# Delta-rule branch of a two-layer decoder step: which side products run whole, where the output products stand between the chain's steps, and the order of four small steps

## The reference

```python
def rwkv7_scan(r, w, k, v, kk, a, S0):
    def step(S, xs):
        r_t, w_t, k_t, v_t, kk_t, a_t = xs
        sa = jnp.einsum('bhvk,bhk->bhv', S, -kk_t)
        S = (S * w_t[:, :, None, :] + sa[..., None] * (kk_t * a_t)[:, :, None, :]
             + v_t[..., None] * k_t[:, :, None, :])
        y = jnp.einsum('bhvk,bhk->bhv', S, r_t)
        return S, y
...
    y = head_groupnorm(y, ln_w, ln_b)
    y = y + jnp.sum(r_h * k_h * rk, axis=-1, keepdims=True) * v_h
    return y.reshape(B, T, RWKV_W) * g, S, p_rwkv[:, -1, :]
```

## Time and profile before

| | |
|---|---|
| median of 3 runs | 2676.49 us (2673.93 to 2677.24) |
| the profiled execution's own time | 2676.28 us |
| its span in the trace | 2674.5 us |
| TensorE busy | 2612.9 us, 98% of the span |
| VectorE busy | 846.5 us, 32% |
| ScalarE busy | 581.3 us, 22% |
| delta stage, layer 0 | 415 to 741 us of the span |
| delta stage, layer 1 | 1497 to 1823 us |
| TensorE's waits for L1588 (`bonus_sum`) | 5.1 us in 14 waits |
| TensorE's waits for L1662 (`level_w`) | 4.1 us in 18 waits |
| one middle pass of the loop | 39.5 us (x 12; the first and the last pass of each layer differ) |

### The profile page before, as it was taken

How to read it: one execution, slowest core, us unless ns; L and a number is a source line. 1 busy time by engine, 2 the same in 40 slices (tenths; PEclk the granted TensorE clock), 3 DMA queues, 4 the chain that set the end, 5 groups by cost and what they waited for, 6 DMA issues and landing times. The chain is left out here.

```text
span 2674.5 us, 81765 instructions
## 1 busy us (share of the span) xinstructions
PE 2612.9 (98%) x36178; PEld 2063.5 (77%) x36178; DVE 846.5 (32%) x2419; ACT 581.3 (22%) x1731; POOL 0.2 (0%) x4
## 2 busy tenths in 40 slices
PE   8999999999999999999999999999999999999998
PEld 5777886666677777677777666667799999999997
DVE  2022665556511000202266556561311111111111
ACT  2232333333211000112333333321111111111111
POOL 0000000000000000000000000000000000000000
PEclk9999999999999999999999999999999999999999
DMA  6333442222243434342354222223499999999997
GB/s 220 115 128 131 129 157 82 74 70 72 88 139 121 138 130 140 106 140 74 119 179 153 89 70 72 78 96 112 160 390 385 370 378 393 378 370 383 391 369 277
DMA packets 145547, 499.14 MB, mean 187 GB/s; under 512 B 18736, under 2 KB 23472, under 8 KB 142800
## 3 DMA queue, kind: packets, MB, share of 16 engines
q1 hardware_dynamic: 145360, 496.43, 52.2%
HBM read 476.07 MB, written 20.29 MB: 186 GB/s over the span
## 5 line engine op out<-in xcount | busy, mean ns | idle before, releaser
L407 PE MATMUL psum<-work,ring 128*64 128x88 f32 x11264 | 434.5, 239 | 3.6 <-issue 3.6
L407 PEld LDWEIGHTS psum<-work,ring 128*64 128x64 f32 x11264 | 432.9, 136 | 5.9 <-issue 5.8
L315 PE MATMUL psum<-hT,ring 128*128 128x288 f32 x1536 | 405.0, 411 | 0.0
L315 PEld LDWEIGHTS psum<-hT,ring 128*128 128x128 f32 x1536 | 280.9, 190 | 73.3 <-ACT work L418 2.7
L2158 PE MATMUL psum<-work,proj 128*64 128x88 f32 x5632 | 223.7, 239 | 1.5 <-issue 1.5
L2158 PEld LDWEIGHTS psum<-work,proj 128*64 128x64 f32 x5632 | 218.3, 136 | 6.2 <-issue 6.2
L400 PE MATMUL psum<-hT,ring 128*128 128x288 f32 x768 | 187.1, 406 | 0.0
L1449 ACT ACTIVATE work<-psum 128x256 f32<-128x256 f32 (+4 forms) x304 | 102.6, 371 | 386.2 <-PE psum L1360 97.8
L400 PEld LDWEIGHTS psum<-hT,ring 128*128 128x128 f32 x768 | 145.8, 190 | 40.9 <-issue 0.8
L1874 PE MATMUL psum<-hT,ring 128*128 128x288 f32 x704 | 172.5, 409 | 1.7 <-DVE hT L1953 1.7
L293 PE MATMUL psum<-hT,ring 128*64 128x288 f32 x1104 | 165.8, 418 | 0.0
(11 more groups left out here) (440 smaller groups left out, 3041.9 us busy)
## 6 DMA issues: line engine op xcount, KB each, us to landing
ring<-w_ff_dram SPq DMA_DIRECT2D x420, 512.0 KB, 6.5
ring<-w_mix_dram SPq DMA_DIRECT2D x256, 512.0 KB, 3.8
proj<-w_ff_dram SPq DMA_DIRECT2D x128, 512.0 KB, 5.3
proj<-w_ff_dram SPq DMA_DIRECT2D x64, 384.0 KB, 5.5
work<-s_gla_dram SPq DMA_DIRECT2D x8, 1024.0 KB, 5.0
gla_s_out<-work SPq DMA_DIRECT2D x8, 1024.0 KB, 4.6
work<-s_ret_dram SPq DMA_DIRECT2D x8, 512.0 KB, 4.8
ret_s_out<-work SPq DMA_DIRECT2D x8, 512.0 KB, 3.0
```

What stands on the lines that cost most here:

```text
L315: mm = (in_halves if self.narrow else nc.tensor.matmul)(out, ring[:, s, k, :], rhs[:, k, :], start=(k == 0), stop=(k == KT - 1))
L407: mm = nc.tensor.matmul(out[64 * c:64 * c + 64], ring[:, s, k, 64 * c:64 * c + 64], rhs[:, k0 + k, :], start=(k0 + k == 0), stop=(k0 + k = ...
```

## The change

Five things, all in the delta stage:

1. Whether a side product is narrow is now said at each `fill`. After the four transposes (`values_to_tokens`, and those of b, k and a) and in the stretch ahead of the loop the products are whole; elsewhere they stay narrow.
2. `output_early` moves from behind `carry` to between `chain(i, 1)` and `chain(i, 2)`. The fills between the chain's steps (2, 1 and 1) go; 3 stand ahead of the chain and 3 behind `output_state`.
3. `bonus_sum(i + 1)` moves from ahead of `level_x(i, 4)` to behind it.
4. On VectorE `centre(i - 1)` moves behind `level(i, 0)`, and `sample_states(i)` moves ahead of `to_chunk_end` and `clear_inverse`.
5. In the last pass a `fill(n)` emits (n + 1) // 2 products in place of one.

```diff
-        def __init__(self, slabs, begun=0, narrow=False):
-            self.narrow = narrow
+        def __init__(self, slabs, begun=0):
+            self.narrow = False
...
-        def __call__(self, n):
+        def __call__(self, n, narrow=False):
+            self.narrow = narrow
             for _ in range(n):
                 next(self.products, None)
...
-                def fill(n):
-                    side(n if more else 1)
+                def fill(n, narrow=True):
+                    side(n if more else (n + 1) // 2, narrow)
...
                 values_to_tokens(i)
-                fill(1)
+                fill(1, narrow=False)
                 level_w(i, 1)
                 b_to_tokens(i)
-                fill(2)
+                fill(2, narrow=False)
                 level_x(i, 1)
...
                 k_to_tokens(i)
-                fill(2)
+                fill(2, narrow=False)
                 level_w(i, 2)
                 a_to_tokens(i)
-                fill(2)
+                fill(2, narrow=False)
                 level_x(i, 2)
...
                 level_w(i, 4)
                 fill(2)
+                level_x(i, 4)
                 if more:
                     bonus_sum(i + 1)
-                level_x(i, 4)
...
                 carry(i)
+                fill(3)
+                chain(i, 1)
                 output_early(i)
-                fill(2)
-                chain(i, 1)
-                fill(1)
                 chain(i, 2)
                 sample_state(i)
-                fill(1)
                 chain(i, 3)
                 output_state(i)
-                fill(2)
+                fill(3)
...
             for i in range(KT):
                 more = i + 1 < KT
+                level(i, 0)
                 if i:
                     centre(i - 1)
-                level(i, 0)
...
                 final_state(i)
+                sample_states(i)
                 if more:
                     to_chunk_end(i + 1)
                     clear_inverse(i + 1)
-                sample_states(i)
-                if more:
                     start_inverse(i + 1)
```

More of the change, by code:

```diff
@@ L1154, in _ @@
                             for i in range(KT) for j in range(4)]
-                           + [(lambda n=n: out_wait(n), n, SIDE_BANK[n][:, 0:T], hT) for n in range(OUT_EARLY)], begun=SIDE_BEGUN, narrow=True)
+                           + [(lambda n=n: out_wait(n), n, SIDE_BANK[n][:, 0:T], hT) for n in range(OUT_EARLY)], begun=SIDE_BEGUN)
             def lora_up(i):
```

## The result

The changed kernel takes 2657.34 us (median of 3 runs, 2656.84 to 2657.67). Against the kernel before, the ratio is 0.993, with a 95% interval of 0.9908 to 0.9953. That is 19.2 us less; the forecast was 2653, 23.5 less, with 2647 to 2662 as its range.

What follows compares the result with a forecast made beforehand. TensorE, busy 38.88 of 39.47 us a middle pass, was taken as the bound. Six passes of 1.61 plus 1.1 and 0.9 gave 11.7 a layer, 23.4 in both: 2653 us, range 2647 to 2662.

Steps and rivals of the forecast that it cites:

- whole products, three places at 0.20: Whole side products behind transposes at levels 1 and 2 save a change of tile: 0.60 us a middle pass.
- `level_w(i, 1)`, order and whole product: With masked copies ahead of `centre`, L1249 no longer waits for VectorE and starts 0.51 us earlier.
- `bonus_sum` behind `level_x`: At level 4 the move trades one wait for nearly the same: 0.05 us, between 0 and 0.36.
- output stretch: From `carry` to `scores`: 0.56 us less work and switching, 0.21 more waiting, net 0.35 a pass, bounds 0 and 0.56.
- `sample_states`: Moved ahead of six small VectorE steps, it ends earlier and frees `scores_rest`: 0.1 us a pass at most.
- part 1: Whole products behind transposes: a place saves 0.15 + 0.05 = 0.20 us, bounds 0.10 and 0.30.
- Ahead of the loop: Stretch before the delta stage's passes: one change of tile comes and a little goes, counted as 0.
- The first and the last pass: Savings of 1.1 us in the first pass and 0.9 in the last, where whole-product savings were halved.
- Whole products worth nothing: Rival: the change to 64*64 behind whole products eats the 0.15; 12 us less gain, 2665 us; chance 0.10.
- The chain laid bare: Rival: small products cover less of the chain's waits, output stretch nets zero; 2658.5 us; chance 0.12.
- the slower case with round trips counted on top: Rival: round trips of 0.66, 0.66 and 0.93 waited for in full; some 7 us slower, 2683; chance 0.02.
- one like price for each change of tile: Reading of the tiling page: every change costs alike, saving only 0.15 a place, 9.6 us over 64 places.

Runs made afterwards that it cites:

- narrow_stage: Changed kernel with all side products narrow in the delta stage alone, including ahead of the loop: 2661.93 us, 0.9949 of the kernel before; middle pass 38.62.
- centre_first: Changed kernel with `centre` again ahead of the first masked copies on VectorE: 2663.07 us, 0.9947 of the kernel before; middle pass 38.47.
- bonus_first: Changed kernel with the bonus sum again ahead of the last level's X products: 2658.09 us, one run; middle pass 38.10.
- old_output: Changed kernel with the output stretch in its old order, fills of 2, 1, 1 and 2: 2664.24 us, 0.9952 of the kernel before; middle pass 38.36.
- bare_chain: Changed kernel with `sample_state` moved from between second and third chain step to behind `output_state`: 2662.65 us, one run; middle pass 38.49.
- all_whole: Changed kernel with every side product whole: 2663.47 us, one run; middle pass 38.64.
- all_narrow: Changed kernel with every side product narrow, also in the two stages ahead of the delta stage: 2692.51 us, 1.006 of the kernel before.
- late_table: Changed kernel with ScalarE's table load moved behind the last level's copy of W: 2651.39 us, 0.9908 of the kernel before; middle pass 37.67.

## Why the prediction was right, and where it was off

The mechanism held part by part, and the direction and size with it. In us per middle pass:

| step of the prediction | forecast | measured |
|---|---|---|
| whole products, three places at 0.20 | 0.60 | 0.44, three quarters of narrow_stage's 0.59 for four places |
| `level_w(i, 1)`, order and whole product | 0.51 | 0.45 between the two profiles (2.23 to 1.78); 0.44 in centre_first |
| `bonus_sum` behind `level_x` | 0.05 | 0.07 (bonus_first) |
| output stretch | 0.35 | 0.33 (old_output) |
| `sample_states` | 0.10 | 0 alone; 0.15 with the old output stretch |
| sum | 1.61 | 1.45 between the two profiles; the rows above, with the 0.15, make 1.44 |

**The term that was mis-sized is part 1.** The prediction put the saving at 0.20 a place: "two should take 0.22". It took 0.11 for each transpose from four of them at 312.29, which followed other 128*128 work. In the delta stage they follow 64*64 work, and a group costs 0.05 more there: 0.27 for two. The trace of the kernel before has this price elsewhere too: the same L751 group takes 0.45 behind 128*128 products, but 0.55 behind 128*32 ones. TensorE's timeline before:

```profile
309.47 0.71 PE L751 MATMUL psum<-work 128*128 128x128 f32 x4
310.02 2.11 PE L315 MATMUL psum<-hT,ring 128*128 128x288 f32 x8
```

So the change to narrow products cost 0.10 at the transposes and not 0.15, and a place saves 0.15, halfway between the forecast and its lower bound of 0.10. At four places a pass that is 0.20 too much in the forecast, part of it in the 0.51 of `level_w(i, 1)`. A price has to be taken from a row with the same neighbours on both sides.

**Ahead of the loop**, "one change of tile comes and a little goes, 0", it was 0.32 us a layer slower (19.03 to 19.35), 0.6 in all. narrow_stage has 19.03 again, so it is the whole products there that cost it; the prediction gave no reason for its 0.

**The first and the last pass** came out at 1.08 and 0.93 less, against 1.1 and 0.9. For the last pass that is partly luck. Undoing one part alone makes it 0.30 (narrow_stage), 0.46 (centre_first) and 0.80 us longer (old_output), 1.56 together: the parts don't add up there, and the output stretch counts for more than twice the 0.35 that the prediction kept. Part 5 lies in the same pass and stays untested. One sign that the prediction named as its being wrong came true there: ScalarE's copies hold `level_x`, 0.26 us at two places, so the transposes with their one product take 1.19 as with a narrow one (5.33 to 6.52 us behind the pass's first L1249 before, 5.34 to 6.53 after), and the whole product saves nothing.

**The whole.** Each delta stage is 10.4 us shorter where 11.7 was forecast, 20.8 in all. The span is only 19.4 shorter: ahead of the delta stages 0.4 us are gained, between and behind them 1.8 are lost, where the change touches nothing. No run was made on these, and they are about as large as the spread of a kernel's own runs; this part stays open.

**The rivals.** Whole products worth nothing: refuted by narrow_stage. The chain laid bare, and the slower case with round trips counted on top: refuted by old_output and bare_chain; the round trips were 0.64 and 0.89, against 0.66 and 0.93 from the rows. With one like price for each change of tile, the nine groups of all_whole between 64*64 products should have cost nothing; they cost 0.05 each. The 0.15 a place that such a price gives did come out, though as 0.10 at the transposes and 0.05 at the products. The Trainium skill, TensorEngine Tiling (Array Packing), Tiling Modes, says that a change of tiling mode drains TensorE; it gives no price, and that the prices are alike was the prediction's own reading of it. The profiles here agree that a change costs time (0.14 for a narrow group between 64*64 products) and show that the price depends on the pair.

**`sample_states`** was in the sum as an additive term and is not one. The 0.1 was gone by the output stretch already. The prediction read the distance of 0.15 us between VectorE's end and L1201 rightly as a wait, but didn't ask what the other part of the change did to it.

## What to carry to other kernels

When an engine is busy for 98% of the time, measure from start to start, and look for what a group costs beyond its arithmetic: here most changes of the tile's shape. Choose the form of filler work by its neighbours, the same shape as what it stands beside, and put it in few large groups, as long as VectorE's or ScalarE's round trips stay covered by small work of the neighbours' shape. Before moving a step away from a wait, ask what its successor waits for; and undo edits in pairs too, since two of them may hide the same wait (the output order and `sample_states`) or may each need the other (the bonus sum and the table load).

## What the runs showed of the hardware that was not expected

- A group of 128*64 products between 64*64 ones costs about 0.28 us beyond its arithmetic: 0.14 at the group (1.12 for two products and 1.61 for three, at 0.49 each) and 0.14 at the small products behind it (0.61 in place of 0.47). Taking two such groups away gave 0.33 and not 0.56, with the chain's waits in it. From 128*128 to 128*64 the change costs 0.10 on the one and 0.05 on the other side. Whole products between 64*64 neighbours cost 0.05 us a group more than narrow ones (1.17 against 1.12), and 0.15 less behind transposes.
- Narrow products in the two stages ahead of the first delta stage, where most neighbours are 128*128 tiles, cost 13.4 us (all_narrow): 5.9 at themselves and 7.9 at the 128*128 work beside them.
- ScalarE's table load costs here what its row says and nothing beside: the sigmoids end at 529.93, the load runs from 529.94 to 531.22, and the copy behind it starts at 531.24. The Trainium skill, ScalarE: Activation LUTs, What ACT_TABLE_LOAD costs, gives the same 1283 ns for the load and adds a drain of about 1380 ns for every switch to another set of tables. By these two figures of the Trainium skill the copy would have started near 532.6, an estimate; it started at 531.24, so no such drain shows here, nor in late_table, where a copy ends at 530.24, the load runs from 530.26 to 531.54 and the next activation starts at 531.55.
